# Modulation rows in rounds of 2048 columns spread over four stages, retention with values centred ahead, and the spatial gate's bias as one product of 256 columns

## The chip, the cores and the metric

One core of a Trainium2 chip runs the whole program; the other cores are idle. The metric is the device time of one execution in microseconds (us), lower is better. The engines of the core are TensorE (PE: matrix products, with PEld for its weight loads), VectorE (DVE), ScalarE (ACT), GpSimd (POOL) and SyncE (SP), which here only issues transfers.

## The reference

Two transformer blocks of depth 2 run one after the other on 256 tokens of width 1024, all in float32. The first has forgetting attention ("fox"), a mixture of 32 experts, retention ("ret"), and a second mixture of experts. The second takes the first's output as x and a context of 256 tokens; both go through mLSTM mixers and gated feed-forward layers, and every one of these is modulated. What the change touches is this:

```python
# modulation, for each layer l of the second block; c and c_ctx are vectors of 1024
mod  = (silu(c)     @ w_mod[l] + b_mod[l])      # w_mod[l]: 1024 x 6144 (24 MB)
modc =  silu(c_ctx) @ w_mod[l] + b_mod[l]
sh1, sc1, g1, sh2, sc2, g2 = split(mod, 6)
px = (rmsnorm(x, norm1_g[l]) * (1 + sc1) + sh1) @ w_in[l] + b_in[l]
...
x = x + g1 * (y_x @ w_out[l])
x = x + g2 * swiglu(rmsnorm(x, norm2_g[l]) * (1 + sc2) + sh2, ...)

# retention, 4 heads, key width 256, value width 512, 256 positions
o = sum of decayed scores times v                # per head
mu = mean(o, axis=-1);  var = mean((o - mu)**2, axis=-1)
o = (o - mu) * rsqrt(var + EPS) * gn_gain
out = (silu(gate) * o) @ w_out

# spatial gate, in each mixer: 2 chunks of 128 positions, 4 groups of 64 channels
mixed = einsum('gpq,bnqgc->bnpgc', w_s, vg) + b_s.T[:, :, None]
y_b = u * mixed
```

## The kernel before, in words

The program is a list of stages: `fox`, `moe(0)`, `ret`, `moe(1)`, then for each layer of the second block a mixer and a feed-forward layer of x ("mix01", "ffn01", "mix11", "ffn11", where the digits are the layer and 1 for x), and `final`. Every engine runs its own instruction stream through all stages, in the order in which the code writes it; engines meet at semaphores only. The context's mixer and feed-forward layer, and the part of the second mixer that leaves only states, run beside the experts in `moe(0)` and `moe(1)`.

Every large product is a `Gemm`. Its weights come in loads of 1 MB; a load is converted in two halves, ACT makes a rounded high part (L401) and DVE the rest, the low part (L412), and PE forms three products for each pair of tiles (L463), each of 256 or 512 columns. A Gemm's halves pass through three to five pairs of buffers, so ACT and DVE work a few halves ahead of PE. The loads of all stages go through one ring of slots (five to eight slots of 1 MB in the stages spoken of here) which SP fills in program order (L248): a load is issued when the work that used its slot is done, and SP waits there, so a slot that comes free late also holds up all later loads. PSUM has eight banks, handed out in turn; a bank can be held until a sum is complete.

`Modulation` (L789) computes, for one layer, all 6144 columns. It runs in `fox` for layer 0 and in `ret` for layer 1, in 12 rounds of 512 columns. `cs` holds the two activated vectors (context and x) as columns in a 32-wide tile for each of the 8 blocks of 128 inputs. A round takes two loads of 1 MB, each of 4 blocks by 512 columns, so each run of memory is 2 KB. For each block PE multiplies in its own group of 32 array columns (L824), so the four results of a round lie in the four quarters of a bank's partitions; ACT copies the bank (L847, `mod_row`), and PE turns it into columns with four small products against `sel2` (L836), which sums the quarters. A product in full float32 stands in the trace as two rows, so L824 has 16 rows for a round and L836 has 8. DVE adds the bias (L866), and after the last round `gains_dve` makes the norm gains of the layer (L855). `pe(i)`, `act(i)` and `dve(i)` are called with step i: PE does round i and turns round i-1.

In `fox` the attention works in 12 batches of heads (4 of them with four heads, 8 with two heads), a step of the loop each, in software pipeline: PE scores of batch i (L980, L982), PE turns the weights of i-1 (L992), PE values of i-2 (L1006), and then the modulation's step. DVE adds the bias and takes the maximum (L1194, L1199, L1201), ACT takes the exponential (L1115), DVE divides (L1182, L1184) in the next step. DVE's step ends with the modulation's bias.

In `ret` the loop `schedule` goes over four heads: scores of head h+1 (L1955, L1957), `centre(h)`, two steps of the modulation, values of head h+1 (L1970 to L1972), `norm_(h)`, a third step. ACT copies the values out of PSUM (L2011), PE sums them over the head (`centre`, L1981), DVE subtracts the mean (L2071), ACT squares (L2019), PE sums the squares (`var`, L1981 too), ACT takes the root (L2024), DVE the reciprocal (L2080), two products (L2081, and L2084 with gain and gate), ACT the high part (L2027), DVE the low part (L2088). Then `ret_out` begins.

In a mixer `sgu_pe` (L2289) forms, for each of two output halves, four products of 128 columns over 128 rows and 64 array columns (L2297), each followed by its bias as a product over 2 rows and 128 columns (L2298). `conv_sum_pe` (L2286) waits for the convolution on DVE at the item `ln_at`, item 17 in mix01.

## Time and profile before

| | |
|---|---|
| median of three runs | 2448.04 us (2442.11 to 2448.26) |
| the profiled execution's own time | 2446.2 us |
| its span in the profile | 2444.4 us |
| PE busy | 2204.5 us, 90% of the span |
| PE weight loads busy | 1782.0 us, 73% |
| DVE busy | 1122.8 us, 46% |
| ACT busy | 886.9 us, 36% |
| POOL busy | 51.1 us, 2% |
| mean TensorE clock granted | 0.94 of full |
| transfers | 676 MB, 277 GB/s over the span |

The span is the time from the first to the last instruction of the profiled execution; its own time lies 1.8 us above it. Busy times of PE are modelled and overlap, so the start times in the timeline tell more than the durations. A row of the timeline gives start, length, engine, line, operation, output and input, the count of merged instructions, and in brackets the idle time before it and who ended it.

### The profile page before, as it was taken

How to read it: one execution, taken by the hardware profiler on the slowest of the kernel's cores; microseconds unless marked ns; L12 is line 12 of the kernel's file. 1: busy time of each engine (PE TensorE's matmuls, PEld its weight loads, DVE VectorE, ACT ScalarE, POOL GpSimd, SP SyncE). 2: the span in 40 equal slices, each digit the busy share in tenths (PEclk: the TensorE clock that was granted, in tenths of full speed). 3: DMA queues.
4: the chain of work that ended last, by engine and by line, in shares of the span. 5: the costliest groups of instructions: out<-in, count | busy, mean ns of one | idle time of the engine just before them, and what ended most of it. 6: DMA issues, size and time to landing. Idle time of an engine off the chain costs nothing. (4 is left out here: it accounts for less than half of the span.)

```text
span 2444.4 us, 45087 instructions
## 1 busy us (share of the span) xinstructions
PE 2204.5 (90%) x19490; PEld 1782.0 (73%) x19490; DVE 1122.8 (46%) x1982; ACT 886.9 (36%) x1491; POOL 51.1 (2%) x94
## 2 busy tenths in 40 slices
PE   7998798998796999879999998978888998898999
PEld 7967466765464996867777775636678998777999
DVE  5355335433523634453333333524765555746554
ACT  4444242133212443332222222324344444444443
POOL 0000000000000000000000000000000000000001
PEclk9999899998998999989999999988889999988999
DMA  7494899999999558659999999897314545413551
GB/s 282 155 342 167 351 426 405 395 410 421 423 421 360 182 184 311 240 214 394 398 412 407 401 410 422 337 425 255 122 44 145 175 159 177 138 35 121 182 172 44
DMA packets 138928, 676.27 MB, mean 277 GB/s; under 512 B 10592, under 2 KB 10848, under 8 KB 76512
## 3 DMA queue, kind: packets, MB, share of 16 engines
q1 hardware_dynamic: 130048, 614.77, 65.4%
q0 software_dynamic: 8672, 58.50, 6.0%
q8 instruction: 159, 2.61, 0.4%
q14 instruction: 49, 0.40, 0.0%
HBM read 672.17 MB, written 1.05 MB: 275 GB/s over the span
## 5 line engine op out<-in xcount | busy, mean ns | idle before, releaser
L463 PE MATMUL bank<-xx,high 128*128 128x256 f32 (+1 forms) x3296 | 630.0, 292 | 35.0 <-DVE xx L624 22.5
L463 PEld LDWEIGHTS bank<-xx,high 128*128 128x128 f32 (+1 forms) x3296 | 520.6, 193 | 90.3 <-issue 60.9
L463 PE MATMUL bank<-xx,low 128*128 128x256 f32 (+1 forms) x1648 | 473.0, 287 | 0.0
L463 PEld LDWEIGHTS bank<-xx,low 128*128 128x128 f32 (+1 forms) x1648 | 319.2, 194 | 1.5
L412 DVE TENSOR_TENSOR low<-lane,high 128x1024 fp32r<-128x1024 f32 (+1 forms) x112 | 130.7, 1170 | 307.1 <-ACT high L401 307.0
L401 ACT ACTIVATE high<-lane 128x1024 fp32r<-128x1024 f32 (+1 forms) x112 | 113.1, 1014 | 291.9 <-PE bank L463 291.9
L463 PE MATMUL bank<-hx,high 128*128 128x256 f32 x1056 | 197.1, 288 | 0.0
L463 PEld LDWEIGHTS bank<-hx,high 128*128 128x128 f32 x1056 | 164.1, 191 | 16.1 <-issue 15.2
L463 PE MATMUL bank<-hx,low 128*128 128x256 f32 x528 | 149.0, 282 | 0.0
L1438 ACT ACTIVATE hs<-bank 64x256 f32<-64x256 f32 x64 | 24.1, 377 | 269.4 <-PE bank L1425 269.3
L463 PE MATMUL bank<-gth,high 128*128 128x256 f32 x384 | 111.6, 291 | 6.9 <-DVE gtl L622 5.2
L1445 DVE TENSOR_TENSOR hs<-hs,bank 64x256 f32<-64x256 f32 x64 | 27.1, 423 | 188.3 <-ACT hs L1438 187.9
L463 PE MATMUL bank<-gtl,high 128*128 128x256 f32 x384 | 110.3, 287 | 0.0
L463 PE MATMUL bank<-gth,low 128*128 128x256 f32 x384 | 110.2, 287 | 0.0
L463 PE MATMUL bank<-high,xx 128*128 128x256 f32 (+1 forms) x416 | 108.8, 343 | 0.9 <-DVE low L412 0.9
L463 PEld LDWEIGHTS bank<-hx,low 128*128 128x128 f32 x528 | 100.9, 191 | 0.0
L463 PEld LDWEIGHTS bank<-high,xx 128*128 128x128 f32 x416 | 75.8, 202 | 17.8 <-issue 8.0
L1425 PE MATMUL bank<-ring__16,xt 128*32 128x256 f32 x1008 | 70.8, 400 | 14.1 <-DMA ring__16<-in_expert_gu_blocks 11.0
L412 DVE TENSOR_TENSOR low<-ring__16,high 128x1024 fp32r<-128x1024 f32 x45 | 54.9, 1225 | 59.8 <-ACT high L401 59.7
L412 DVE TENSOR_TENSOR low<-ring__15,high 128x1024 fp32r<-128x1024 f32 (+1 forms) x46 | 54.1, 1181 | 59.5 <-ACT high L401 59.4
L463 PEld LDWEIGHTS bank<-gth,high 128*128 128x128 f32 x384 | 75.4, 196 | 7.6 <-DVE low L412 7.4
L463 PE MATMUL bank<-xh,high 128*128 128x256 f32 x256 | 74.7, 292 | 6.7 <-DVE low L412 3.5
(575 smaller groups left out, 4083.2 us busy)
## 6 DMA issues: line engine op xcount, KB each, us to landing
ring__16<-in_expert_gu_blocks SPq DMA_DIRECT2D x63, 1024.0 KB, 10.2
ring__50<-in_expert_gu_blocks SPq DMA_DIRECT2D x32, 1024.0 KB, 13.5
ring__14<-in_expert_gu_blocks SPq DMA_DIRECT2D x32, 1024.0 KB, 10.0
ring__15<-in_expert_gu_blocks SPq DMA_DIRECT2D x32, 1024.0 KB, 11.7
ring__14<-in_expert_down_blocks SPq DMA_DIRECT2D x32, 1024.0 KB, 7.7
ring__15<-in_expert_down_blocks SPq DMA_DIRECT2D x32, 1024.0 KB, 8.7
ring__149<-in_expert_gu_blocks SPq DMA_DIRECT2D x32, 1024.0 KB, 9.9
ring__150<-in_expert_gu_blocks SPq DMA_DIRECT2D x32, 1024.0 KB, 10.6
```

Of the source, the lines that this page charges most:

```text
L401: act.activation(self.split_parts(it)[0].bitcast(F32R), src, ACT.Copy).then_inc(*hi.up(it["key"]))
L412: dve.tensor_tensor(low.bitcast(F32R), src, high, SUB).then_inc(*lo.up(it["key"]))
L463: done = pe.matmul(out, a.bitcast(F32R), b.bitcast(F32R), start=it["start"] and k == 0 and q == 0 and not halves, stop=stop)
L1425: i = pe.matmul(bank[32 * h:32 * h + 32, 0:256], xg[:, k, b % GB, :], w[:, k % 2, 256 * h:256 * h + 256], start=k == 0, stop=k == KC - 1, ...
L1438: act.activation(hs[0:64, :], pq[K("up", b)][0:64, 0:256], ACT.Silu).then_inc(*up_a.up(K(b)))
L1445: dve.tensor_tensor(hs[0:64, :], hs[0:64, :], pq[K("up", b)][64:128, 0:256], MUL).then_inc(*up_v.up(K(b)))
```

## The change

`Modulation` now takes a list of (layer, round) pairs. A round has 2048 columns, three to a layer, and is made of 8 units. A unit is one load of 1 MB (one block of 128 inputs by 2048 columns, runs of 8 KB) and four products of 512 columns, in the four groups of array columns; the bank is held over the 8 units. So a layer still has 24 loads and 96 products. After a round there is one copy by ACT and one turn by PE, four products against 8 columns of the identity. The activated vectors are computed once, in `fox` (`silu_act`, kept in `c_silu`), and POOL writes `cs` in each stage. The gains of norm1 and norm2 are made with their rounds. The six rounds are spread: `fox` does (0,0) and (0,1), 16 units over 12 steps; `ret` does (0,2) and (1,0), 16 units over 10 steps; mix01 does (1,1) and the first four units of (1,2), with four units right behind the norm's sums, four in front of `conv_sum_pe` at `ln_at` and a turn three items later, and four in front of the transposes `yt`; ffn01 does the last four units behind the norm's sums, and a turn after item 1. The loads of these units stand between those of the stages' own weights in SP's order. In `ret` the values are centred in the projection (row sums by ACT's eviction, `v_sum`, and three DVE instructions for each head), so that `centre`'s column sums, DVE's subtraction and ACT's copy are gone; ACT squares straight from PSUM, DVE applies gain and gate straight from PSUM (`gate`), and the reciprocal root is multiplied in afterwards. The order of the loop is changed. In `sgu_pe` two bias products of 256 columns for each half come first, ahead of the wait, and the four products follow.

```diff
+def __init__(self, name, room, rounds, first=0, row=None, cs=None, steps=12):
+    self.name, self.room, self.steps = name, room, steps
+    self.units = [(L, r, k) for L, r in rounds for k in range(KC)][first:]
+    self.cs = room("cs", KC, 32) if cs is None else cs
+    self.rows = Turns([room("mod_row", 512) if row is None else row], kept)
+def ends(self, i):
+    return [self.units[u][:2] for u in self.at(i) if self.units[u][2] == KC - 1] if i >= 0 else []
+def at(self, i):
+    n, m = len(self.units), self.steps
+    return range(min(n, -(-n * i // m)), min(n, -(-n * (i + 1) // m)))
+def sp(self, sp, units):
+    for L, r, k in units:
+        ring.load(sp, ("mod", L, r, k), self.room, A["w_mod_2"][L, k * P:(k + 1) * P, SLOT * r:SLOT * (r + 1)], 1, SLOT)
+def silu_act(self, act):
+    act.activation(c_silu[:, :, 0], V("cc"), ACT.Silu)
+    act.activation(c_silu[:, :, 1], V("c"), ACT.Silu).then_inc(*mod_row.up("silu"))
+def setup_pool(self, pool):
+    pool.memset(self.cs, 0.0).then_inc(*mod_set.up((self.name, "zero")))
+    pool.wait_ge(*mod_set.at((self.name, "zero")))
+    pool.wait_ge(*mod_row.at("silu"))
+    pool.tensor_scalar(self.cs[:, :, 0:2], c_silu, 1.0, None, MUL).then_inc(*mod_set.up(self.name))
+def unit_pe(self, pe, unit):
+    L, r, k = unit
+    key = ("mod", L, r)
+    pe.wait_ge(*mod_set.at(self.name))
+    if k == 0:
         banks.next(key)
+        banks.hold(key)
+        for s, q in banks.freed(key):
+            pe.wait_ge(*s.at(q))
+    w = ring.view(self.room, ("mod", L, r, k), 4, 512)
+    pe.wait_ge(*ring.ready(("mod", L, r, k)))
+    for j in range(4):
+        n = pe.matmul(banks[key][32 * j:32 * j + 32, :], self.cs[:, k, :], w[:, j, :], start=k == 0, stop=k == KC - 1,
+                      tile_position=(0, 32 * j))
+    n.then_inc(*mod_mm.up((L, r, k)))
+    ring.free(("mod", L, r, k), (mod_mm, (L, r, k)))
+    if k == KC - 1:
+        banks.release(key)
+def row_act(self, act, L, r):
+    row = self.rows.next((L, r))
+    act.wait_ge(*mod_mm.at((L, r, KC - 1)))
+    for s, q in self.rows.freed((L, r)):
+        act.wait_ge(*s.at(q))
+    act.activation(row, banks[("mod", L, r)][:, :], ACT.Copy).then_inc(*mod_row.up((L, r)))
+    banks.free(("mod", L, r), (mod_row, (L, r)))
+def turn_pe(self, pe, L, r):
+    key, row = ("turn", L, r), self.rows[(L, r)]
+    banks.next(key)
+    for s, q in banks.freed(key):
+        pe.wait_ge(*s.at(q))
+    pe.wait_ge(*mod_row.at((L, r)))
+    used = ident.rearrange("p (a b) -> p a b", a=4)[:, :, 0:2]
+    for j in range(4):
+        n = pe.matmul(banks[key][:, 8 * j:8 * j + 8], row[:, j * P:(j + 1) * P], used, start=True, stop=True)
+    n.then_inc(*mod_turn.up((L, r)))
+    self.rows.free((L, r), (mod_turn, (L, r)))
+def out_dve(self, dve, L, r):
+    key = ("turn", L, r)
+    mod = mods[:, 128 * L:128 * L + 96].rearrange("p (c v) -> p c v", v=2)
+    gm = mods[:, 128 * L + 96:128 * L + 128].rearrange("p (i c v) -> p i c v", i=2, c=8)
+    dve.wait_ge(*mod_turn.at((L, r)))
+    dve.tensor_tensor(mod[:, 16 * r:16 * r + 16, :].rearrange("p (j c) v -> p j c v", j=4),
+                      banks[key][:, 0:32].rearrange("p (c j v) -> p j c v", c=4, j=4),
+                      bc(V("b_mod", 48 * L + 16 * r, 16).rearrange("p (j c) -> p j c", j=4), [P, 4, 4, 2], 3), ADD).then_inc(
+        *mod_out.up((L, r)))
+    banks.free(key, (mod_out, (L, r)))
+    if r == 1:
         return
+    i, nm, sc = ((0, "norm1", 8), None, (1, "norm2", 32))[r]
+    dve.wait_ge(*mod_out.at((L, r)))
+    dve.scalar_tensor_tensor(gm[:, i], mod[:, sc:sc + 8, :], 1.0, bc(V(nm, 8 * L, 8), [P, 8, 2], 2), ADD, MUL).then_inc(
+        *gm_v.up((L, i)))
+def step_pe(self, pe, i):
+    for u in self.at(i):
+        self.unit_pe(pe, self.units[u])
+    for L, r in self.ends(i - 1):
+        self.turn_pe(pe, L, r)
+def step_act(self, act, i):
+    for L, r in self.ends(i):
+        self.row_act(act, L, r)
+def step_dve(self, dve, i):
+    for L, r in self.ends(i - 1):
+        self.out_dve(dve, L, r)
...
-mod = Modulation(0, room)
+mod = Modulation("fox", room, [(0, 0), (0, 1)])
...
-    for i in range(12):
-        mod.sp(sp, i)
+    mod.sp(sp, mod.units)
...
-    mod.setup_act(act)
+    mod.silu_act(act)
...
-sq = tmp[:, 4:8, :]
+mod = Modulation("ret", room, [(0, 2), (1, 0)], steps=10)
+sq_b = Turns([tmp[:, 0:4, :], tmp[:, 4:8, :]], kept)
+v_sum = room("v_sum", 4, 2)
...
-        norm.done, moving=False, a=lambda e, a, o, n, ps: e.activation(v[:, a, o:o + n], ps, ACT.Copy)),
+        norm.done, moving=False,
+        a=lambda e, a, o, n, ps: e.activation(v[:, a, o:o + n], ps, ACT.Copy, accum_out=v_sum[:, o // 512, a:a + 1])),
...
-    for i in range(12):
-        mod.sp(sp, i)
+    mod.sp(sp, mod.units)
...
     values(0)
-    at = 0
     for h in range(4):
         if h < 3:
             scores(h + 1)
-        centre(h)
+        gate(h)
         step(3 * h)
-        step(3 * h + 1)
         if h < 3:
             values(h + 1)
+        step(3 * h + 1)
         norm_(h)
         step(3 * h + 2)
...
+        pe.wait_ge(*vc_v.at(h))
...
+    def var(h):
+        key, sq = ("var", h), sq_b[h]
         pe.wait_ge(*rv_a.at((h, 2)))
+            n = pe.matmul(bank[:, 0:T], ones, sq[:, i, :], start=i == 0, stop=i == 3)
+        n.then_inc(*rn_p.up(h))
+        sq_b.free(h, (rn_p, h))
...
         for e in range(0, 4, 2):
             act.wait_ge(*rv_p.at((h, e)))
-            act.activation(o_[:, e:e + 2, :], banks[("rv", h, e)][:, :].rearrange("p (a t) -> p a t", a=2), ACT.Copy).then_inc(
+            act.activation(sq[:, e:e + 2, :], banks[("rv", h, e)][:, :].rearrange("p (a t) -> p a t", a=2), ACT.Square).then_inc(
...
+    def centre(h):
+        dve.wait_ge(*ev_a.at(proj.out(2, 512 * h, 1)))
+        dve.tensor_scalar(v_sum[:, h, :], v_sum[:, h, :], -1.0 / 512, None, MUL).then_inc(*vc_v.up((h, "mean")))
+        dve.wait_ge(*vc_v.at((h, "mean")))
+        for a in range(2):
+            z = v[:, a, 512 * h:512 * h + 512]
+            n = dve.tensor_scalar(z, z, v_sum[:, h, a:a + 1], None, ADD)
+        n.then_inc(*vc_v.up(h))
+        for h in range(4):
+            if it["at"] == proj.last[2, 512 * h] + 1:
+                centre(h)
...
+    def gate(h):
+        for e in range(0, 4, 2):
+            dve.wait_ge(*rv_a.at((h, e)))
+            for j in range(2):
+                c = 4 * h + e + j
+                n = dve.scalar_tensor_tensor(gt[:, c, :], banks[("rv", h, e)][:, j * T:(j + 1) * T], gn[:, c:c + 1], gt[:, c, :], MUL, MUL)
+            n.then_inc(*rv_v.up((h, e)))
+            banks.free(("rv", h, e), (rv_v, (h, e)))
...
         seq = in_order(dve, v_step, ("ret", h))
         seq(dve.reciprocal(rs, rs))
-        seq(dve.tensor_tensor(o_, o_, bc(rs, [P, 4, T], 1), MUL))
-        for e in range(4):
-            j = 4 * h + e
-            n = dve.scalar_tensor_tensor(gt[:, j, :], o_[:, e, :], gn[:, j:j + 1], gt[:, j, :], MUL, MUL)
-        n.then_inc(*rn_v.up(h))
-        o_b.free(h, (rn_v, h))
+        dve.wait_ge(*rv_v.at((h, 2)))
+        dve.tensor_tensor(gt[:, hs, :], gt[:, hs, :], bc(rs, [P, 4, T], 1), MUL).then_inc(*rn_v.up(h))
         dve.wait_ge(*o_h.at(("ret", h)))
         dve.tensor_tensor(gtl[:, hs, :].bitcast(F32R), gt[:, hs, :], gth[:, hs, :], SUB).then_inc(*o_l.up(("ret", h)))
...
+if cs is not None:
+    mod = Modulation(name, room, [(1, 1), (1, 2)], row=kn[:, 0].rearrange("p h d -> p (h d)"), cs=cs)
...
+    if mod:
+        mod.sp(e, mod.units[0:1])
+        proj.loads(e, 0, 2)
+        mod.sp(e, mod.units[1:2])
+        proj.loads(e, 2, 4)
+        mod.sp(e, mod.units[2:4])
+        proj.loads(e, 4, 16)
+        mod.sp(e, mod.units[4:8])
+        proj.loads(e, 16, len(proj.items))
+        outp.loads(e, 0, 4)
+        mod.sp(e, mod.units[8:12])
+        outp.loads(e, 4, len(outp.items))
+        return
...
-    pe.wait_ge(*sgu_v.at(K("shift")))
     for c in cs:
         bank = take(pe, bk, K("sgu", c))
+        for g in (2 * c, 2 * c + 1):
+            q0 = 64 * (g % 2)
+            rows = bc(R("sgub", 512 * L + g * P, P)[0].bitcast(F32), [2, 2, P], 1)
+            pe.matmul(bank[q0:q0 + 64, 0:T], ones[96:98, 0:64], rows, start=True, stop=False, tile_position=(96, q0))
+        pe.wait_ge(*sgu_v.at(K("shift")))
         for a in range(2):
             for g in (2 * c, 2 * c + 1):
                 q0 = 64 * (g % 2)
-                o = bank[q0:q0 + 64, a * P:(a + 1) * P]
-                pe.matmul(o, sv[:, a, g * 64:(g + 1) * 64], wst[:, g, :], start=True, stop=False, tile_position=(0, q0))
-                n = pe.matmul(o, ones[96:98, 0:64], R("sgub", 512 * L + g * P, P)[0].bitcast(F32), start=False, stop=True,
-                              tile_position=(96, q0))
+                n = pe.matmul(bank[q0:q0 + 64, a * P:(a + 1) * P], sv[:, a, g * 64:(g + 1) * 64], wst[:, g, :], start=False, stop=a == 1,
+                              tile_position=(0, q0))
...
+    if mod:
+        for unit in mod.units[0:4]:
+            mod.unit_pe(pe, unit)
...
+        if mod and at == ln_at:
+            for unit in mod.units[4:8]:
+                mod.unit_pe(pe, unit)
+        if mod and at == ln_at + 3:
+            mod.turn_pe(pe, 1, 1)
...
+    if mod:
+        for unit in mod.units[8:12]:
+            mod.unit_pe(pe, unit)
...
+            if mod and at == ln_at:
+                mod.row_act(act, 1, 1)
...
-    dve.wait_ge(*gm_v.at(L))
+    dve.wait_ge(*gm_v.at((L, 0)))
+    if not states_only:
+        dve.wait_ge(*mod_out.at((L, 1)))
...
+        if mod and at == ln_at + 4:
+            mod.out_dve(dve, 1, 1)
...
+mod = Modulation(name, room, [(1, 2)], 4) if v and not L else None
...
+    if mod:
+        mod.sp(e, mod.units[0:1])
+        up.loads(e, 0, 2)
+        mod.sp(e, mod.units[1:2])
+        up.loads(e, 2, 4)
+        mod.sp(e, mod.units[2:4])
+        up.loads(e, 4, len(up.items))
...
+    if mod:
+        for unit in mod.units:
+            mod.unit_pe(pe, unit)
+    for it in up.pe(pe):
+        if mod and it and it["at"] == 1:
+            mod.turn_pe(pe, 1, 2)
...
+    if mod:
+        up.act_high(act, 3)
+        mod.row_act(act, 1, 2)
...
+        if mod and it["at"] == 2:
+            mod.out_dve(dve, 1, 2)
```

## Rows read from the trace of the kernel before

**Rows 1.** The page's moved bytes in 40 slices of the span, GB/s in each.

```profile
GB/s 282 155 342 167 351 426 405 395 410 421 423 421 360 182 184 311 240 214 394 398 412 407 401 410 422 337 425 255 122 44 145 175 159 177 138 35 121 182 172 44
```

**Rows 2.** Windows (us, busy by engine, clock, DMA): ret's attention, mix01's spatial gate.

```profile
918.00:994.00 76.00, 66.41 (x482) 44.57 (x483) 34.70 (x70) 26.84 (x41) 0.00 (x0) 0.96 0.88 332
...
1760.00:1768.00 8.00, 8.00 (x23) 5.05 (x23) 1.97 (x2) 1.76 (x2) 0.00 (x0) 0.50 0.28 115
```

**Rows 3.** Timeline of PE, one step of fox's attention with two heads.

```profile
155.22 0.70 PE L980 MATMUL bank<-kt,qt 64*128 64x256 f32 x2
...
158.12 1.06 PE L824 MATMUL bank<-ring__18,cs 128*32 128x512 f32 x8
...
159.97 1.05 PE L836 MATMUL bank<-sel,mod_row 128*128 128x2 f32 x8
160.96 0.70 PE L980 MATMUL bank<-kt,qt 64*128 64x256 f32 x2
```

**Rows 4.** Timeline of DVE and ACT, four heads, then two heads, and the end.

```profile
124.12 0.40 ACT L1115 ACTIVATE tmp<-tmp,rs 128x128 f32<-128x128 f32 x1 [0.97 <-DVE rs L1201]
...
128.69 0.40 ACT L1115 ACTIVATE tmp<-tmp,rs 128x128 f32<-128x128 f32 x1 [2.45 <-DVE rs L1201]
...
155.41 0.15 DVE L1182 RECIPROCAL rs<-rs 128x2 f32<-128x2 f32 x1
...
156.62 0.88 DVE L1194 SCALAR_TENSOR_TENSOR tmp<-bank,rs,vec 128x256 f32<-128x256 f32 x2 [0.34 <-PE bank L982]
...
159.37 0.19 ACT L1115 ACTIVATION_READ_ACCUMULATOR tmp<-tmp,rs 128x1 f32 x1
...
187.17 0.51 ACT L1115 ACTIVATE scores<-scores,rs 128x256 f32<-128x256 f32 x1 [3.49 <-DVE rs L1201]
```

**Rows 5.** Groups by line in ret's attention: count, busy, mean ns, idle before.

```profile
L2080 DVE RECIPROCAL rs<-rs 128x256 f32<-128x256 f32 x4 | 7.0, 1752 | 16.8 <-ACT rs L2024 16.8
...
L2088 DVE TENSOR_TENSOR gtl<-gt,gth 128x1024 fp32r<-128x1024 f32 x4 | 4.9, 1224 | 4.5 <-ACT gth L2027 4.5
...
L2027 ACT ACTIVATE gth<-gt 128x1024 fp32r<-128x1024 f32 x4 | 4.2, 1056 | 19.1 <-DVE gt L2084 19.1
...
L2011 ACT ACTIVATE tmp<-bank 128x512 f32<-128x512 f32 x4 | 2.4, 597 | 6.8 <-PE bank L1972 6.8
...
L2024 ACT ACTIVATE rs<-bank,vec 128x256 f32<-128x256 f32 x4 | 1.9, 474 | 4.8 <-PE bank L1981 4.8
```

**Rows 6.** Timeline of PE in ret: start, values, column sum, last turn, ret_out.

```profile
918.36 1.13 PE L1955 MATMUL bank<-qt,kt 128*128 128x256 f32 x4 [0.47 <-ACT gt L1911]
...
931.05 0.47 PE L1970 MATMUL bank<-st,v 128*128 128x128 f32 x2
...
933.81 1.89 PE L1981 MATMUL bank<-tmp,vec 128*128 128x256 f32 x8
935.63 1.07 PE L824 MATMUL bank<-ring__14,cs 128*32 128x512 f32 x8
...
990.05 1.84 PE L836 MATMUL bank<-sel,mod_row 128*128 128x2 f32 x8 [4.15 <-ACT mod_row L847]
...
993.57 0.58 PE L463 MATMUL bank<-gth,high 128*128 128x256 f32 x1 [1.69 <-DVE low L412]
```

**Rows 7.** Timeline of PE, its waits in mix01 and at ffn01's start.

```profile
1747.12 2.04 PE L2286 MATMUL bank<-tm,vec 128*128 128x256 f32 x4 [7.56 <-DVE tm L2691]
...
1824.22 0.63 PE L2421 MATMUL bank<-vec,hn 128*128 128x128 f32 x4 [1.47 <-DVE hn L2905]
...
1828.40 0.77 PE L463 MATMUL bank<-xx,high 128*128 128x256 f32 x2 [2.23 <-DVE xx L2913]
...
1857.86 0.77 PE L463 MATMUL bank<-xx,high 128*128 128x256 f32 x2 [5.04 <-DVE xx L624]
```

**Rows 8.** Timeline of PE, the spatial gate in mix01 from first to last.

```profile
1756.26 0.43 PE L2297 MATMUL bank<-wst,tm 128*64 128x128 f32 x2
...
1763.83 2.08 PE L2286 MATMUL bank<-tm,vec 128*128 128x256 f32 x4
```

142 lines of the change are left out of this document (25 added, 117 removed).

## The prediction

> **What bounds the kernel now.** I read first the page's slices with the moved bytes. Between 250 and 1650 us two long stretches move 395 to 426 GB/s; they are the two mixtures of experts, and transfers bound them [rows 1]. What the change does to PE there is worth nothing. Everywhere else the bytes are far below that, so the order of instructions decides. Next I read the two attentions as windows and as timelines.
>
> In fox's attention PE never rests between two steps: a step with two heads runs from 155.22 to 160.96, 5.74 us, of which the modulation takes 1.85 for its products and 0.99 for its turn; without both 2.90 are left [rows 3]. DVE and ACT together need less: from the reciprocal at 155.41 to the last exponential's end at 159.56 there are 4.15, of which 0.34 are a wait for PE; with about 0.1 of hand-over a lap of DVE and ACT is 3.9 us. With four heads this lap is 4.57 (124.12 to 128.69) [rows 4].
>
> In ret's attention PE is busy 66.4 of 76 us at a granted clock of 0.96 [rows 2]; the 75.2 us from 918.36 to 993.57 [rows 6] are PE's own work and, at the ends of heads, a chain through ACT and DVE.
>
> **Part by part: fox.** The products stay what they are: 1.85 us per round of 512 columns is 0.925 for a unit [rows 3]. There were 12 rounds with 12 turns; there are 16 units with 2 turns. A step with two heads is 2.90 + 16/12 x 0.925 = 4.13 us on PE, just above the lap of 3.9 of DVE and ACT. A step with four heads goes by the lap of 4.57. The exponential of the first batch stays at 124.12; three laps of 4.57 reach 137.8, one mixed step of about 4.2 reaches 142.0, seven of 4.13 reach 170.9. Before it was 187.17 [rows 4]: 16 us less. The tail after it stays, since the same turn stands in it. In the first steps PE will wait for the lap of DVE and ACT, and after such gaps the clock may be down for some microseconds; I take 13, with 8 and 16 as ends. The copy into `mod_row` on ACT and the bias on DVE leave ten of twelve steps; both lie inside the lap's waits and I count them at nothing. POOL's three instructions for `cs` replace DVE's and ACT's; POOL has nothing else at that time, and 120 us of projection hide them. The 16 loads instead of 24 leave SP's queue 8 MB shorter before `out_proj`; it had room before, nothing gained.
>
> **ret.** Gone from PE are four column sums of 1.82 (933.81 to 935.63) [rows 6], eleven of twelve turns net of two new ones (about ten times 0.95), and 8 of 24 units (7.4): together 24 us. But then PE is no longer the bound; the chain is. I write it out from the rows. The first stretch to the end of `var(0)`: scores 1.4, decay 0.9, values 2.8 (931.05 to 933.81), scores 1.3, two units 1.8, values 2.8, two units 1.8, sum of squares 1.8: 14.6. After it a lap runs from one `var` to the next: root 0.5, reciprocal 1.8, product 1.2 (as L2088, same size), copy 1.1, low 1.2 [rows 5], then DVE's decay 0.7, which values wait for, values 2.8, one or two units 0.9, sum of squares 1.8: 12.0. Two laps bring `var(2)` to 38.6. Then 5.8 for root to low. Meanwhile ACT makes the last squares (1.2, two of 0.6 as L2011 [rows 5]) and only then the row of (1,0), behind its copy of head 2; PE's turn of that round stands ahead of `var(3)`: it ends at 47.9. Root to low again 5.8 gives 53.7, and the first low part of `ret_out`'s weights, which stands behind, 1.2: PE begins `ret_out` at 54.9 after 918.36, where it was 75.2. That is 20 less. New gaps of 2 to 7 us open on PE (after each `scores`, before `var(3)`), and before such gaps went with half clock: 993.57 came after waits of 4.15 and 1.69. I take 18, with 8 and 22 as ends. DVE's gate products (four for each head, reading PSUM instead of the copy) stay four; they stand before the reciprocal, in DVE's wait. The unit loads have 5 slots and 16 MB in 50 us; that is 320 GB/s, below the 395 to 426 of [rows 1], so no wait, and if one, the far end 8 contains it.
>
> Where values are centred ahead: ACT's eviction now reads its accumulator (0.19 in fox [rows 4], 8 times, under PE's products of the same projection), and DVE has three instructions for each head, two of 512 columns. The nearest row is the decay or a bias of 256 columns at 0.88 for two [rows 4], so at most 1 us a head, between low parts of the weights. DVE is 46% busy and runs halves ahead there. At nothing; if this cover were thin it would cost at most 4 us, and the end of 8 holds it too.
>
> **The spatial gate.** In mix01 it ran from 1756.26 to 1763.83, 7.57 us [rows 8], at a granted clock of 0.50 with PE busy the whole 8 us [rows 2]. Half of its products are biases with 128 columns, each with its own change of array position. Eight products of four positions become four of twice the columns, ahead of the wait. I take half the time back, 4 us in each of mix01 and mix11. Bounds: 0, if it is the changes of position that cost and the reversed order loses what it won, and 6 if the new bias products fall entirely into the wait ahead. So 8 of 0 to 12. The same edit in the two stages beside the experts is under transfers.
>
> **The units that move to mix01 and ffn01.** Sixteen units of 0.925 are 14.8 us of PE, and two turns are 2. Where they lie: four behind the norm's sums, where PE waits for DVE's norm; four at `ln_at`, where it waits 7.56 for the convolution (3.7 of it then used); four at `yt`, where waits of 1.47 and 2.23 stand; four at ffn01's start, where it waits 5.04 [rows 7]. Hidden are the first, second and fourth. The third uses 3.7 in place of waits of 1.47 and 2.23, which come from a chain through DVE that does not shorten; but not both are ahead of it, so I put 2.0 on it. The turns stand in PE's own stream: 1.0 each, 2.0. In return PE is busy in two gaps after which the clock was down: I take 1.0 at `ln_at` and 1.5 at ffn01. Together +1.5, from -2 to +8. Behind the wait for a unit's load stand all later products of PE; the 16 loads take about 2.5 us each at 410 GB/s, 41 us in total, and the slices there show 122 to 177 GB/s [rows 1]. There is room for them twice over. They stand before each stage's own weights in SP's queue, so the first weights of a stage come 2.5 us later for each unit ahead, one or two units; prefetch across the stage's edge covers it. ACT in ffn01 now copies the row ahead of its high parts; `up.act_high` for three halves is put ahead of that. The bank of a unit is held over the gap from mix01 to ffn01: seven banks are left to turn, and no row shows a wait for a bank that this could lengthen.
>
> **The sum.** fox -13, ret -18, the spatial gate -8, the moved units +1.5: -37.5 us. The profiled execution took 2446.2 us, so it would take 2408.7. The median of the runs is 1.8 above it, so 2411.
>
> **The rivals.** *The chains give less.* PE's work leaves but clock gaps and laps of DVE and ACT that I took too short eat half: fox -8, ret -10, gate -4, moved units +1.5 with their turns: -20.5, some 2427. Against it: the terms of the laps are all rows; for it: the half clock after gaps, seen in [rows 2, 6]. *The moved work is exposed.* The loads of units come late or the four units of `yt` and ffn01 lie open: eight units 7.4, and 4 for weights that came later; the rest as forecast: -27.5 or so, 2421. *It gives more.* The lap in fox is bound by nothing but 3.9, the chain in ret overlaps one unit more, the gate gives 12: -50, 2398. *The change does not do what it says.* If the turns had not been on PE's path at all, fox would keep its 5.74; [rows 3] with no idle time on PE excludes it.
>
> *The clock falls through both attentions: slower.* PE gets less dense there than it was. At 0.50 a two-head step on PE would be 8.3 instead of 5.74, 2.5 more in each of eight, and about 8 in the rest: fox +28. ret's remaining PE work of some 42 us becomes 84 against 75.2, +10. With the gate's -8 and the moved units' +1.5 as they are: +31.5, about 2479. Between the forecast's -37.5 at full clock and this, the win is gone from 37.5 / 69, some 54% of the attentions' time at half clock, a mean of 0.73; before it was 0.96 [rows 2] with far fewer gaps. The Trainium skill, "TensorE: Matmul & The Clock Gate", section "Loop structure matters more than you think", sketches a loop in which a long wait ahead of every product makes PE go cold, and one with products back to back in which it stays warm. By that rule the gaps of ret are where it would show; the trace agrees insofar as the half clock of [rows 2] stands in a stretch with gaps before it, but PE there also recovered within a few microseconds of steady work.
>
> **How the numbers follow.** Forecast 0.64, less from the chains 0.13, moved work exposed 0.04, more 0.09, all terms at their bad ends (-8, -8, 0, +8: -8, or 2440) 0.05, slower 0.05. The likeliest is 2411. The range of 2396 to 2428 takes in "more", "exposed" and nearly all of "less". The measurement can tell about 0.3%, 7.3 us. Every case but the last two ends further than that below 2448: faster 0.90; the bad ends together lie at its edge, same 0.05; slower 0.05.
>
> **What would show it.** In the profile after: fox's steps with two heads at 4.1 to 4.3 and the last exponential near 171; ret from its first score to `ret_out` in 55 to 58, with PE waiting on `rs` and DVE busy; the spatial gate near 4 us; mix01 to ffn11 some 7 us shorter in all; waits on ring slots nowhere above 1 us. The prediction is wrong if the clock in the attentions' windows is below 0.85, if the lap of DVE and ACT grows (reads of PSUM by DVE's gate beside PE's writes), or if waits for slots appear in front of L824 or L463.

## The result and the profile after

The changed kernel takes 2412.15 us (median of four runs, 2409.59 to 2417.00) against 2447.32 us of the kernel before: ratio 0.986, 95% interval 0.9845 to 0.9878. The forecast was 2411, within 2396 to 2428. The time was right; two of its terms were far off, in opposite directions, and the experiments below show where.

In the page of the changed kernel, the span and the moved bytes in 40 slices:

```profile
span 2407.5 us, 44639 instructions
...
GB/s 287 158 278 136 377 425 410 423 424 425 405 421 331 185 175 279 193 278 397 394 405 408 410 409 424 330 425 294 187 78 243 177 159 183 140 47 116 190 168 43
```

The mixtures still move about 400 GB/s, and the late stages have room, as in [rows 1].

To find where 36.9 us of span went (2444.4 less 2407.5), I took the start of the same PE instruction in both timelines and subtracted, at the edges of stages. This shift (after less before) reads:

| place on PE | shift, us | change in the stretch |
|---|---|---|
| fox's attention begins | +0.2 | |
| its `out_proj` begins | -12.9 | -13.1 |
| ret's attention begins | -16.1 | -3.2 |
| `ret_out` begins | -31.6 | -15.5 |
| mix01's gate GEMM, late | -32.7 | -1.1 |
| behind the column sum at `ln_at` | -33.9 | -1.2 |
| ahead of the spatial gate, mix01 | -28.3 | +5.6 |
| behind the gate and the products that ran at half clock | -36.3 | -8.0 |
| last products of mix01 (a turn lies between) | -35.3 | +1.0 |
| behind ffn01's first products | -30.1 | +5.2 |
| ahead of the spatial gate, mix11 (a turn lies between) | -28.9 | +1.2 |
| behind it | -36.9 | -8.0 |
| end | -36.9 | 0.0 |

Fox, in PE's timeline of the changed kernel (a row: start, length, engine, line, operation, output and input, count, and in brackets the idle time before it and who ended it): one step with one unit, one with two.

```profile
159.86 0.70 PE L1001 MATMUL bank<-kt,qt 64*128 64x256 f32 x2
...
162.81 1.07 PE L833 MATMUL bank<-ring__17,cs 128*32 128x512 f32 x8
163.81 0.70 PE L1001 MATMUL bank<-kt,qt 64*128 64x256 f32 x2
...
167.72 1.04 PE L833 MATMUL bank<-ring__19,cs 128*32 128x512 f32 x8
168.69 0.70 PE L1001 MATMUL bank<-kt,qt 64*128 64x256 f32 x2
```

The steps take 3.95 and 4.88 us where [rows 3] had 5.74, and no wait stands between them. Two other steps with two heads are longer: one of 5.74 us holds two units and the turn, and one of 5.35 us ends in a wait that was not there before:

```profile
150.09 0.70 PE L1001 MATMUL bank<-kt,qt 64*128 64x256 f32 x2 [1.34 <-ACT mod_row L845]
```

The scores of a batch wait for ACT's copy of the modulation's row, which they don't read. It is the first and smallest of three such waits.

Retention, PE's waits from the first score to `ret_out`, and the window over it (length, busy time of PE, PEld, DVE, ACT and POOL with counts, granted clock, share of DMA, GB/s):

```profile
902.31 1.13 PE L1971 MATMUL bank<-qt,kt 128*128 128x256 f32 x4 [0.47 <-ACT gt L1928]
...
923.95 0.80 PE L1987 MATMUL bank<-st,v 128*128 128x128 f32 x2 [2.14 <-DVE st L2080]
...
950.33 1.03 PE L856 MATMUL bank<-vec,mod_row 128*128 128x8 f32 x8 [3.54 <-ACT mod_row L845]
951.21 3.66 PE L2000 MATMUL bank<-tmp,vec 128*128 128x256 f32 x8
...
961.97 0.58 PE L464 MATMUL bank<-gth,high 128*128 128x256 f32 x1 [7.09 <-DVE low L413]
```

```profile
902.00:962.00 60.00, 45.42 (x305) 29.56 (x305) 27.16 (x42) 15.34 (x24) 0.00 (x0) 0.91 0.73 280
```

59.66 us, where [rows 6] had 75.21. PE is busy 45 of 60 us, and its waits end with DVE or, once, with ACT's copy of the row: the chain sets the end now, as forecast. But the last sum of squares (L2000) takes 3.66 us behind a wait of 3.54 us; elsewhere it takes 1.99. The values behind the wait of 2.14 us take 4.5 us (923.95 to 928.42), those of the next head 2.9. The granted clock of the whole stretch was 0.96 before [rows 2] and is 0.91 now; it is 0.62 from 923.9 to 928.4 and 0.57 from 951 to 955.

The spatial gate of mix01 in PE's timeline:

```profile
1727.93 0.65 PE L2323 MATMUL bank<-row,vec 2*64 2x256 f32 x4
1728.51 0.66 PE L2328 MATMUL bank<-wst,tm 128*64 128x128 f32 x8
...
1730.26 1.13 PE L2314 MATMUL bank<-tm,vec 128*128 128x256 f32 x4
```

2.33 us where [rows 8] had 7.57, and the column sum behind it takes 1.13 instead of 2.08: the granted clock there is 1.00, that is 2.4 GHz, where it was 0.50. Of the 8.0 us in the table, 5.2 lie in the gate and 2.8 in the products behind it.

And two larger waits that were not there. PE at `ln_at` and at ffn01's start, then ACT at the same two places:

```profile
1714.47 1.10 PE L2314 MATMUL bank<-tm,vec 128*128 128x256 f32 x4 [3.98 <-DVE tm L2734]
...
1721.48 0.80 PE L464 MATMUL bank<-high,xx 128*128 128x512 f32 x1 [3.66 <-ACT kn L845]
...
1829.19 0.76 PE L464 MATMUL bank<-xx,high 128*128 128x256 f32 x2 [8.15 <-ACT mod_row L845]
```

```profile
1720.32 0.63 ACT L2489 ACTIVATE tm<-tm 128x512 f32<-128x512 f32 x1 [11.95 <-DVE tm L2742]
1720.85 0.58 ACT L845 ACTIVATE kn<-bank 128x512 f32<-128x512 f32 x1
...
1828.52 0.58 ACT L845 ACTIVATE mod_row<-bank 128x512 f32<-128x512 f32 x1
```

The units themselves are hidden: the wait for the convolution fell from 7.56 [rows 7] to 3.98, by the 3.5 us that four units take. But the projection's next product waits until ACT has copied the round's row; it starts within 0.1 us after the copy's end in both places. ACT had been idle for 11.95 us at `ln_at`; its copy stood behind the convolution's activation.

### The profile page after: what moved, and what is told of

It reads as the page before. It is cut to its first block and busy times, and to the rows that moved or that the text cites. A ratio compares the mean times of both kernels' runs of the same rounds, so it can differ in the third digit from the quotient of the medians.

```text
span 2407.5 us, 44639 instructions
## 1 busy us (share of the span) xinstructions
PE 2157.5 (90%) x19290; PEld 1745.7 (73%) x19290; DVE 1118.9 (46%) x1956; ACT 872.1 (36%) x1475; POOL 53.6 (2%) x102
## 3 DMA queue, kind: packets, MB, share of 16 engines
q1 hardware_dynamic: 111616, 614.77, 66.2%
## 5 line engine op out<-in xcount | busy, mean ns | idle before, releaser
L464 PEld LDWEIGHTS bank<-hx,high 128*128 128x128 f32 x1056 | 164.1, 191 | 16.1 <-issue 15.2
L1522 PE MATMUL bank<-tmp,y 32*128 32x256 f32 x1024 | 82.4, 440 | 1.4 <-DVEq L1610 1.1
L413 DVE TENSOR_TENSOR low<-ring__16,high 128x1024 fp32r<-128x1024 f32 x47 | 57.2, 1225 | 48.7 <-ACT high L402 48.6
## 6 DMA issues: line engine op xcount, KB each, us to landing
ring__14<-in_expert_gu_blocks SPq DMA_DIRECT2D x33, 1024.0 KB, 12.5
```

The lines of the kernel that those rows point to most:

```text
L413: dve.tensor_tensor(low.bitcast(F32R), src, high, SUB).then_inc(*lo.up(it["key"]))
L464: done = pe.matmul(out, a.bitcast(F32R), b.bitcast(F32R), start=it["start"] and k == 0 and q == 0 and not halves, stop=stop)
L1522: i = pe.matmul(acc_b[h][:, j * T:(j + 1) * T], y[32 * h:32 * h + 32, j * P:(j + 1) * P], d[32 * h:32 * h + 32, b % GB, :], start=False, s ...
```

## Experiments

The times are medians, with the ratio to the kernel before run on the same chip and its 95% interval. Medians of nearly equal kernels scatter by some 5 us: single runs of one kernel reach from 2399.8 to 2414.9 (ret_turn, below). So effects of a few us are read from the stretch of the profile in which they lie, and the whole time is used for what is larger.

**The gate alone (gate_only).** The kernel before with the new `sgu_pe`; the diff is that of the change.

> The kernel before with the new spatial gate alone. The forecast's step: half of the gate's time comes back, 4 us in each of mix01 and mix11, nothing beside the experts: -8 us, ratio 0.997. The rival, read from the trace after the change: the gate falls from 7.6 to about 2.4 us at full clock, the products behind it run at full clock too, 8 to 9 us in each mixer, and the stretch of moe(0) in which the context's gate lies gives 4 to 5 us since loads are no longer held up: -20 to -22 us, ratio 0.991 to 0.992.

Measured: 2429.59 us, ratio 0.9937 (0.9914 to 0.9959): -18.6 us by the medians, -15 by the ratio. In the profile the shift is -5.4 us at ret's attention, and it falls by 8.0 across the gate of mix01 and by 8.0 across that of mix11. The forecast's 8 in all lies outside the interval; the rival's account holds stretch by stretch, and its total of 20 to 22 lies at the interval's edge. That a stage bound by transfers gained too shows in the window from 400 to 500 us in `moe(0)` (share of DMA and GB/s last), of the kernel before and of gate_only:

```profile
400.00:500.00 100.00, 93.47 (x930) 68.60 (x931) 41.02 (x73) 21.95 (x39) 2.64 (x5) 0.91 0.95 392
...
400.00:500.00 100.00, 90.75 (x972) 67.25 (x972) 44.48 (x75) 25.77 (x44) 3.17 (x6) 0.97 0.98 406
```

In the kernel before, the 100 us ahead of it and behind it have a share of 1.01 and 1.00; here the queues had room. With the shorter gate they move 3.6% more in the same 100 us. The gain at ret's attention was 5.4 us here and 2.5 and 3.4 us in the next two runs.

**The same products in another order (gate_order), and wide products in the old order (gate_wide).**

```diff
 # gate_order
 for a in range(2):
     for g in (2 * c, 2 * c + 1):
         ...
         pe.matmul(o, sv[:, a, g * 64:(g + 1) * 64], wst[:, g, :], start=True, stop=False, tile_position=(0, q0))
+    for g in (2 * c, 2 * c + 1):
+        ...
         n = pe.matmul(o, ones[96:98, 0:64], R("sgub", 512 * L + g * P, P)[0].bitcast(F32), start=False, stop=True, ...)
```

```diff
 # gate_wide
 for g in (2 * c, 2 * c + 1):
+    pe.matmul(bank[q0:q0 + 64, 0:T], ones[96:98, 0:64], rows, start=True, stop=False, tile_position=(96, q0))
+    for a in range(2):
+        n = pe.matmul(bank[q0:q0 + 64, a * P:(a + 1) * P], sv[...], wst[:, g, :], start=False, stop=a == 1, tile_position=(0, q0))
```

> The kernel before with the same 16 products of 128 columns in the gate, only in another order: two products with data, then their two biases, so that neighbours lie in different halves of the array columns. If it is neighbours in the same columns that wait for each other, the gate takes 3 to 4 us and the kernel gains nearly what the whole edit gives (-15 to -20 us). If number and width of the products set the time, the gate stays at 7.5 us and the kernel at 2447.

> The kernel before with bias products of 256 columns as in the change, but all three products of one half of the array columns in a row, behind the same wait as before. If neighbours in the same columns wait for each other, the gate takes 5 to 6 us, well above the 2.4 of the change. If number and width set the time, it takes about 2.5 us as in the change.

Measured: 2429.50 us, ratio 0.9927 (0.9905 to 0.9948), and 2429.52 us, ratio 0.9929 (0.9902 to 0.9957). PE's timeline of the gate in mix01, gate_order:

```profile
1756.53 0.44 PE L2297 MATMUL bank<-wst,tm 128*64 128x128 f32 x4
1756.90 0.43 PE L2301 MATMUL bank<-row,vec 2*64 2x128 f32 x4
...
1759.46 1.81 PE L2286 MATMUL bank<-tm,vec 128*128 128x256 f32 x4
```

gate_wide:

```profile
1757.20 0.64 PE L2296 MATMUL bank<-row,vec 2*64 2x256 f32 x2
1757.78 0.65 PE L2298 MATMUL bank<-wst,tm 128*64 128x128 f32 x4
...
1761.74 1.11 PE L2298 MATMUL bank<-wst,tm 128*64 128x128 f32 x4
1762.78 2.08 PE L2286 MATMUL bank<-tm,vec 128*128 128x256 f32 x4
```

and of the kernel before, between the two rows of [rows 8]:

```profile
1756.62 0.43 PE L2298 MATMUL bank<-row,vec 2*64 2x128 f32 x2
1756.98 0.43 PE L2297 MATMUL bank<-wst,tm 128*64 128x128 f32 x2
...
1762.60 0.69 PE L2297 MATMUL bank<-wst,tm 128*64 128x128 f32 x2
```

In the kernel before a product (two records) starts every 0.36 us at full clock, so the sixteen would take 5.8 us there; the rest of the 7.57 is half clock. In gate_order two products start in the same 0.36 us, so the gate takes 2.93 us with the same sixteen products. What lets two run side by side is not their different halves of the array columns alone. In the old order the bias at 1756.62 uses the lower half and the product with data at 1756.98 the upper one, and they still start one after the other; these two use different rows of the array (rows 96 and 97 against all 128). The pairs that start together, in gate_order and in the change, use the same rows and different column halves. So the account that gate_order was built on, that neighbours in the same columns wait for each other, is half of it. With wide products in a row the gate takes 5.58 us, more than twice the 2.33 of the change. (In mix01 the clock fell in its last quarter; in mix11 it didn't, and the gate took 4.61 us there, about twice 2.33.) So the order halves the time, and the wide biases take a fifth off it (5.8 to 4.61, 2.93 to 2.33). The whole times of the three variants are equal; by the shifts across the gates of mix01 and mix11 they are not: 8.0 and 8.0 us for the change's gate, 5.8 and 5.8 for gate_order, 2.6 and 5.7 for gate_wide.

**Retention alone (ret_only).** The kernel before with ret's new values, gate and order of the loop, and the old `Modulation`.

> The kernel before with the change of retention alone (values centred ahead, gate products from the bank, new order of the loop), and the modulation in 12 rounds of 512 columns with 12 turns as before. The forecast's account: PE loses 7.3 us of column sums and keeps its rounds and turns, so the attention goes from 75.2 to about 68 us, -7 us, ratio 0.997. The rival: centring took most of ret's gain since it shortened the chain, and the modulation's turns were beside the path: -13 to -16 us, ratio 0.994.

Measured: 2450.10 us, ratio 1.0011 (0.9995 to 1.0026). No gain, and both expectations are wrong. PE's timeline, waits from first score to `ret_out`:

```profile
917.91 1.13 PE L1955 MATMUL bank<-qt,kt 128*128 128x256 f32 x4 [0.47 <-ACT gt L1912]
...
941.20 1.06 PE L824 MATMUL bank<-ring__16,cs 128*32 128x512 f32 x8 [3.09 <-DVE gt L2073]
...
958.91 1.11 PE L824 MATMUL bank<-ring__123,cs 128*32 128x512 f32 x8 [3.09 <-DVE gt L2073]
...
979.34 1.05 PE L836 MATMUL bank<-sel,mod_row 128*128 128x2 f32 x8 [2.13 <-DVE gt L2073]
...
994.70 0.58 PE L463 MATMUL bank<-gth,high 128*128 128x256 f32 x1 [1.69 <-DVE low L412]
```

76.8 us, 1.6 more than before. The column sums' 7.3 us are gone, and in their place products and a turn of the modulation wait 8.3 us for DVE's gate products (L2073), whose output they don't read: what they need is the bank. The values now stay in their bank until DVE's gate has read them, where ACT's early copy had freed it, and a modulation with a bank for every round and turn runs into it. In the changed kernel the modulation needs one held bank and two turns, and no such wait stands in ret.

**The modulation alone in ret (mod_only).** The changed kernel with ret's old values, centring and loop, the new rounds kept.

> The changed kernel with retention's values as before (centring by a column sum in the loop, ACT's copy, DVE's subtraction, the product with the root ahead of gain and gate, the old order of the loop); all else as changed. Retention's change alone gave nothing as long as 24 rounds and turns filled PE. Theory A: with the turns gone the chain of a head bounds the attention, so centring ahead is now worth its column sum, copy, subtraction and second square: ret's attention 8 to 12 us longer than the 59.7 of the change, 2420 to 2424 in all. Theory B: it is beside the path here too, since the modulation's fewer turns gave all of it: ret's attention 60 to 62 us, 2412 to 2414.

Measured: 2414.56 us, ratio 0.9879 (0.9856 to 0.9902). Same view:

```profile
902.89 1.13 PE L1971 MATMUL bank<-qt,kt 128*128 128x256 f32 x4 [0.47 <-ACT gt L1927]
...
970.97 0.58 PE L464 MATMUL bank<-gth,high 128*128 128x256 f32 x1 [8.80 <-DVE low L413]
```

68.1 us, 8.4 more than with both, in the range of theory A; the median says only +2.4 and cannot be used for it. (At ret's attention the profiled execution was within 0.6 us of the changed kernel's; at ffn01 its banks fall otherwise and it has no wait for the row, some 6 us less.) The two parts of ret don't add: -7.1 for the modulation alone, +1.6 for retention alone, -15.5 together. What of retention's part is the centring, what the gate read from PSUM and what the order of the loop is not separated.

**All rounds back in fox and ret (late_back).**

```diff
-mod = Modulation("fox", room, [(0, 0), (0, 1)])
+mod = Modulation("fox", room, [(0, 0), (0, 1), (0, 2)])
-mod = Modulation("ret", room, [(0, 2), (1, 0)], steps=10)
+mod = Modulation("ret", room, [(1, 0), (1, 1), (1, 2)])
```

and no modulation in mix01 and ffn01.

> The changed kernel with all three rounds of a layer where they were before: 24 units over 12 steps in fox and 24 in ret, nothing in mix01 and ffn01. If the move is worth something, fox takes 2 units of 0.925 in each step instead of 1.33, 0.6 us more in each of 12 steps (+7), ret about 8 units on the path (+4 to +7), while mix01 and ffn01 give back 12.7 us: the sum is 2410 to 2414, no gain from the move. The forecast's account, by which the moved units cost only 1.5 us: +10 to +13 us, 2422 to 2425.

Measured: 2408.09 us, ratio 0.9845 (0.9831 to 0.9858). Fox's attention takes 68.2 us (63.1 in the changed kernel), ret's 66.2 (59.7), 11.7 more together; 3.6 us of it are waits of four units in ret for their own loads. mix01 and ffn01 have no loss. The move as the change makes it is worth nothing that the medians can tell (it loses 4 us by them, and the intervals overlap); the forecast's account of it is refuted.

**Whose wait is it: the bank given back later (bank_late), the row copied earlier (rows_early).**

```diff
 # bank_late: unit_pe, turn_pe
-    if k == KC - 1:
-        banks.release(key)
...
     self.rows.free((L, r), (mod_turn, (L, r)))
+    banks.release(("mod", L, r))
```

```diff
 # rows_early: ACT in mix01, ACT in ffn01
+if mod and at == ln_at:
+    mod.row_act(act, 1, 1)
 if at in (ln_at, ln_at + 2):
     conv_ln_act(act, (at - ln_at) // 2)
-if mod and at == ln_at:
-    mod.row_act(act, 1, 1)
...
 up.act_high(act, 2)
+if mod:
+    mod.row_act(act, 1, 2)
 norm.split_act(act)
...
-if mod:
-    up.act_high(act, 3)
-    mod.row_act(act, 1, 2)
```

> The changed kernel, with the bank of a modulation round given back after the turn instead of after the last unit; nothing else moves. Theory A: PE's waits of 3.66 us at ln_at and 8.15 us at ffn01's start, which end with ACT's copy into the row, are there because the released bank is the next in turn, so the next product of the projection gets it. Then both waits shrink to those of before (0 and about 2) and the kernel takes 2403 to 2405, 7 to 9 us less than the changed one. Theory B: PE waits for ACT's other work or for loads, and the copy only ends at the same moment: 2412, no change.

> The changed kernel, with ACT's copy of the row moved ahead: at ln_at in front of the convolution's activation, in ffn01 in front of the norm's split; the bank is given back as in the change. Theory A (PE waits for the bank that the copy frees): as with the late release, 2403 to 2405. Theory B (loads of units or weights are late): 2412; and if the copy in ACT's queue delays the norm, 1 us more.

Measured: bank_late 2402.82 us, ratio 0.9829 (0.9815 to 0.9842); rows_early 2399.45 us, ratio 0.9805 (0.9791 to 0.9818). PE's timeline of bank_late:

```profile
1709.82 2.05 PE L2313 MATMUL bank<-tm,vec 128*128 128x256 f32 x4 [3.98 <-DVE tm L2733]
...
1819.58 0.77 PE L464 MATMUL bank<-xx,high 128*128 128x256 f32 x2 [8.15 <-ACT mod_row L843]
```

and of rows_early:

```profile
1722.22 2.05 PE L2314 MATMUL bank<-tm,vec 128*128 128x256 f32 x4 [3.98 <-DVE tm L2734]
...
1826.72 0.47 PE L464 MATMUL bank<-xx,high 128*128 128x256 f32 x2 [1.73 <-DVE xx L625]
```

At `ln_at` either edit takes the wait away altogether, and bank_late also takes away the 1.34 us in fox, which rows_early doesn't touch. At ffn01 only the earlier copy does (8.15 to 1.73), and the list of PE's instructions with their banks tells why. Of the changed kernel, then of bank_late (what a product waits for in brackets):

```
L833 MATMUL bank4<-ring0__14,cs_270 32x512 x3
L464 MATMUL bank4<-xx_266,high_260 128x256 [waits x_low,mod_row,w_low]

L833 MATMUL bank7<-ring0__14,cs_270 32x512 x3
L464 MATMUL bank7<-xx_266,high_260 128x256 [waits x_low,mod_row,w_low]
```

The first product of `up` gets the very bank in which the round was just summed, since a bank that is given back is taken next when the turn stands at it. In bank_late it should have been held, but the bank happened to be number 7, and `Early` (L704 to L706) sets bank 7 aside for a moment and then strikes it from the set of held banks: the hold was lost. So the mechanism, the bank's next user waiting for ACT's copy, is shown at `ln_at` by two independent edits and at ffn01 by one edit and the list. In the same list, fox's scores that wait 1.34 us get bank 0, in which round (0,0) was just summed. With the copies ahead the move is worth something: 2399.45 us against 2408.09 with all rounds back, and the intervals don't overlap.

**The end of ret (ret_order, ret_turn, fill).** ret_order puts ACT's squares and DVE's gate products of head h+1 ahead of the normalisation of head h; ret_turn moves the last turn too; fill leaves the order and adds products.

```diff
 # ret_order and ret_turn: schedule
 values(0)
+gate(0)
 for h in range(4):
     ...
-    gate(h)
     step(3 * h)
     if h < 3:
         values(h + 1)
+        gate(h + 1)
-    step(3 * h + 1)             # ret_turn only
+    if h < 3:                   # ret_turn only
+        step(3 * h + 1)
     norm_(h)
+    if h == 3:                  # ret_turn only
+        step(3 * h + 1)
     step(3 * h + 2)
```

```diff
 # fill: PE; keep_busy(n) makes n products of 256 columns into a bank of their own
 if h == 2:
+    keep_busy("fill_values", 4)
 pe.wait_ge(*rs_v.at(h))
...
 if i == 10:
+    keep_busy("fill_turn", 7)
 mod.step_pe(pe, i)
```

> The changed kernel; in ret ACT's squares and DVE's gate products of head h+1 stand ahead of the normalisation of head h instead of behind it. If the end of ret is the chain that the forecast wrote out (copy of head 2, squares of 3, row, turn, sum of squares of 3), the squares and the row come about 5 us earlier, and ret is 3 to 5 us shorter: 2407 to 2409. If PE's or DVE's own stream sets the end, there is no change, 2412.

> The changed kernel with the order of the loop as in ret_order and, for the last head, the turn of round (1,0) behind the sum of squares instead of ahead of it. Moving the squares alone gave nothing since the turn still waited for the row, which ACT copies behind the high part of head 2. Theory A (that wait and the half clock after it are the cost): PE goes from the units straight to the sum of squares at full clock, the last reciprocal starts 5 us earlier, 2407 to 2409. Theory B (DVE's own stream of head 2 sets the end): at most 1 us, 2411 to 2413.

> The changed kernel with 4 products of 256 columns added in PE's stream ahead of the values of head 2 and 7 ahead of the turn of (1,0); they read data that lies ready, and nobody reads their bank. They fill PE's waits of 2.1 and 3.5 us. Theory A (the 4.5 us by which ret missed the forecast are half clock after these waits): values of head 2 take 2.8 instead of 4.5 us and the last sum of squares 1.9 instead of 3.7, ret's attention is 2.5 to 3.5 us shorter though PE does more, 2409. Theory B (the clock falls by something else than the waits): no faster, or up to 1 us slower where the added products outlast the waits, 2412 to 2413.

Measured: ret_order 2412.56 us, ratio 0.9860 (0.9845 to 0.9875), ret's attention 59.6 us: no gain, the expectation was wrong. The turn of (1,0) still stood ahead of the sum of squares and still waited for its row. ret_turn 2411.01 us, ratio 0.9860 (0.9838 to 0.9881), fill 2414.00 us, ratio 0.9855 (0.9827 to 0.9882); by the whole time neither is told from the changed kernel. By the stretch they are. PE's timeline of ret_turn:

```profile
899.31 1.13 PE L1975 MATMUL bank<-qt,kt 128*128 128x256 f32 x4 [0.47 <-ACT gt L1928]
...
943.73 1.99 PE L2004 MATMUL bank<-tmp,vec 128*128 128x256 f32 x8
946.36 1.03 PE L856 MATMUL bank<-vec,mod_row 128*128 128x8 f32 x8 [0.64 <-ACT mod_row L845]
953.76 0.58 PE L464 MATMUL bank<-gth,high 128*128 128x256 f32 x1 [6.37 <-DVE low L413]
```

and of fill:

```profile
903.28 1.13 PE L1971 MATMUL bank<-qt,kt 128*128 128x256 f32 x4 [0.47 <-ACT gt L1928]
...
951.38 1.97 PE L2009 MATMUL bank<-tmp,vec 128*128 128x256 f32 x8
...
960.44 0.58 PE L464 MATMUL bank<-gth,high 128*128 128x256 f32 x1 [7.09 <-DVE low L413]
```

ret_turn takes 54.5 us, 5.2 less than the changed kernel. fill takes 57.2, 2.5 less, though PE does more: 0.8 at the values of head 2, and 1.7 where the last sum of squares takes 1.97 again instead of 3.66. So half clock after waits is part of ret's time, shown by filling the waits.

**Put together (best).** The edits of rows_early and ret_turn, and the four added products ahead of the values of head 2.

> The changed kernel with what the other runs showed put together: the row copies ahead as in rows_early (waits for the bank of 5.5 and 5.2 us gone), the order of ret_turn (5.2 us off ret's attention) and the four added products of fill ahead of the values of head 2 alone (1.5 us off). If the gains add up, 10.7 + 5.2 + 1.5 = 17 us below the changed kernel, 2395. If the end of ret's attention is taken by the mixture's transfers behind it, only those of mix01 and ffn01 remain, 2400 to 2402.

Measured: 2394.27 us (2391.92 to 2398.66), ratio 0.9783 (0.9766 to 0.9800), the fastest of all: 54 us below the kernel before, 18 below the change. Ret's attention, in the window over it and in PE's timeline:

```profile
890.00:950.00 60.00, 56.45 (x416) 40.51 (x414) 23.97 (x37) 15.82 (x28) 0.00 (x0) 1.00 0.71 268
```

```profile
903.72 1.13 PE L1975 MATMUL bank<-qt,kt 128*128 128x256 f32 x4 [0.47 <-ACT gt L1928]
...
957.35 0.58 PE L464 MATMUL bank<-gth,high 128*128 128x256 f32 x1 [6.37 <-DVE low L413]
```

53.6 us, with the clock at 1.00 up to the last head. By the medians the gains add up as expected: 17.9 us below the change, 17 expected. The profiled execution was only 12.1 below the changed kernel's: ret gives 6.0 and the two waits 9, and some 3 are given back elsewhere, 1.4 of them ahead of ret. Fox's 1.34 us are still in it (148.65).

## Why the prediction came out right

**Fox: right in mechanism and size.** -13 forecast, -13.1 measured. Steps with two heads take 3.95 us with one unit and 4.88 with two; four of the twelve steps have two units, which averages 4.3, near the 4.13 that the rows gave. The last exponential came 11.3 us earlier (175.83 against 187.17), not the 16 of the sum written out, and the tail behind it, put at nothing, gave 1.5. So the allowance of 3 us met the sum of the two; the wait of 1.34 us for a bank, which the forecast did not have, lies in it. late_back prices the parts: with 24 units and three turns the attention takes 68.2 us (76.1 before), so nine turns less are 7.9 us, and eight units and one turn less 5.1.

**Ret: right in mechanism, the size 2.5 us off.** The chain written out from the rows gave 54.9 us and 57.2 with the allowance; 59.7 were measured. The order of the chain was right; the laps between two roots were 14.0 and 12.7 us where 12.0 was written (ACT's timeline of the changed kernel):

```profile
917.49 0.48 ACT L2029 ACTIVATE rs<-bank,vec 128x256 f32<-128x256 f32 x1 [7.92 <-PE bank L2000]
...
931.45 0.47 ACT L2029 ACTIVATE rs<-bank,vec 128x256 f32<-128x256 f32 x1 [1.30 <-PE bank L2000]
...
944.12 0.47 ACT L2029 ACTIVATE rs<-bank,vec 128x256 f32<-128x256 f32 x1 [7.08 <-PE bank L2000]
```

So 4.8 us came on top of the bare chain, where 2 were allowed. Half clock took 3.3 of them, 1.6 in the values of head 2 (in the lap of 14.0) and 1.7 in the last sum of squares, and fill gave 2.5 back. The other 1.5 are a first stretch and laps that were written 0.4 to 0.7 us too short each. ret_turn comes to 54.5, close to the bare chain, by luck: it still has the long laps, and it gains by another order. The forecast priced ret's parts together only, and so had no step that failed there; its expectation for the part alone, made in the same way, did fail.

**The spatial gate: the step that failed first.** "I take half the time back, 4 us in each of mix01 and mix11", bounds 0 and 6. It was 8.0 in each, and 2.5 to 5.4 more in `moe(0)` in the three gate runs, counted at nothing as "under transfers". Three things were missed: neighbouring products on the same array rows and in different column halves run side by side (gate_order); part of the gate's 7.57 us was half clock; and the column sum and the weights' products behind the gate had run at half clock too (2.8 of the 8.0). In the Trainium skill, "TensorE: Matmul & The Clock Gate", section "Why this matters for your kernels", has a row by which products whose outputs lie in distinct column groups run at the same time; the trace agrees for gate_order, 0.36 us for two products where the old order had 0.36 for one. For neighbours on different rows of the array it does not: distinct column halves alone gave no overlap in the old order. I had read [rows 8] as a cost per instruction.

**The moved units: the step that failed second.** +1.5 forecast, 5.6 at `ln_at` and 5.2 at ffn01 measured. The units were hidden where I put them, and the clock at the column sum of `ln_at` gave back 1.2 us where 1.0 was forecast. But the prediction said of the bank held: "no row shows a wait for a bank that this could lengthen." No row of before could: the wait is for a bank whose reader, ACT's copy, is new and stands deep in ACT's queue. The fault was to look for the wait in the old trace rather than to ask who gets the bank next and what its release waits for. The `yt` units, put at +2.0, cost 0.1 by the shifts (-35.4 ahead of them, -35.3 behind). The two turns cost 0.9 each, where 1.0 was forecast. The queue of loads, the slots, POOL, and the centring under the projection cost nothing that shows, as said: no unit waits 0.8 us or more for its load, and the shift stays at -16.1 through ret's projections.

**The sum.** Forecast: -13 - 18 - 8 + 1.5 = -37.5. Measured: -13.1 for fox, -15.5 for ret, -16.0 for the gates of mix01 and mix11, +11.5 for the moved units (5.6 and 5.2 at the two waits, 1.8 for the turns, 0.1 at `yt`, less 1.2 of clock), -3.2 on the way to ret, and -0.6 in small pieces: -36.9. The surprise of the gate and `moe(0)`, -11.2, nearly cancels that of the moved units and ret, +12.5. The median agrees with the forecast to 1 us by that, not by skill.

**The signs.** Of what the prediction named to look for, the spatial gate near 4 us (2.33), ret in 55 to 58 (59.7), the last exponential near 171 (175.8) and mix01 to ffn11 some 7 us shorter (4.2 by the shifts) did not come; the clock in the attentions (0.97 in fox, 0.91 in ret, limit 0.85) did.

**The rivals.** "The moved work is exposed" had the right place and the wrong mechanism: not loads or units, but a copy. "It gives more" had the gate at 12 us; it gave 16. The clock's fall through both attentions did not come: 0.91 in ret's window, where at 0.73 the win would have been gone. Single waits were followed by half clock, as that rival's ground said.

## What to carry to other kernels

When work is moved into an engine's idle time, follow not only its own run time but its buffer: who is handed it next, and where in which queue the instruction stands that frees it. Two losses of 5 us came from copies of 0.6 us, and only with those copies moved ahead in ACT's order was the move worth anything. And before costing a group of small products by their count, look at which rows and columns of the array each one uses, and at the clock they ran at: at full clock the same sixteen take 5.8 us in one order and 2.93 in another.

A part's worth depends on what stands beside it: retention's part was worth nothing with the old modulation and 8.4 us with the new one, so try a part on both sides of a change.

## What the runs showed of the hardware

Two products of 64 array columns start within 0.01 us of each other when they use the same rows and different column halves (the pairs of gate_order and of the change). When the rows differ too, they start one after the other, 0.36 us apart (bias and data of the old order).

The granted clock fell inside the old gate without any wait close before it. The last wait had ended at 1747.12, and the clock had come back since: products start every 0.36 us from 1756.26 and, from 1759.5 on, every 0.62 us, with PE busy throughout. In gate_wide it fell inside the gate in mix01, at 1760.70, and not at all in mix11 with the same instructions. What decides between the two isn't settled by these runs; the short gates (2.33 and 2.93 us) saw no fall inside them, though in gate_order the column sum behind took 1.81 us in mix01.
